# Encoder layer on one core: order of transfers, splits and down-weight sums at the phase boundaries

## What is computed

```
x = x + concat(attention, pooling) @ w_out        # 1024 -> 1024
h2 = rmsnorm(x, norm2_g)
x = x + square(relu(h2 @ w_up)) @ w_down          # 1024 -> 4096 -> 1024
```

## Time and profile before

| | us |
|---|---|
| timed runs | 1613.30, 1613.46, 1616.38 (median 1613.46) |
| profiled execution, its own time | 1616.33 |
| its span | 1614.5 |
| TensorE busy with matmuls | 1517.9 (94%) |
| DVE, ACT, POOL busy | 1027.1, 728.8, 391.0 |

### The profile page before, as it was taken

One profiled execution on the slowest core, in us unless ns is written; L12 is line 12 of the kernel. 1 busy time (PEld: TensorE's weight loads), 2 busy tenths in 40 slices (PEclk: granted clock), 3 DMA queues, 4 the chain that ended last, 5 costly groups with the idle time before them and its releaser, 6 DMA issues.

```text
span 1614.5 us, 23469 instructions
## 1 busy us (share of the span) xinstructions
PE 1517.9 (94%) x8000; PEld 1343.0 (83%) x8000; DVE 1027.1 (64%) x1290; ACT 728.8 (45%) x1231; POOL 391.0 (24%) x337
## 2 busy tenths in 40 slices
PE   7999989999999987999999999997799999999998
PEld 6999867888778867999999999996587777777777
DVE  6434489999866556345454454466587677687675
ACT  5223279999853334445554454544222223223220
POOL 3423667888830000000000000020211211211200
PEclk9999999999999988999999999999799999999999
DMA  6110021000214638433323333347342342442434
GB/s 223 50 38 17 17 79 34 14 13 10 66 69 182 238 127 322 154 121 141 141 104 145 128 128 135 116 179 266 146 156 88 134 155 80 143 144 90 137 98 169
DMA packets 68789, 193.55 MB, mean 120 GB/s; under 512 B 5504, under 2 KB 7680, under 8 KB 68736
## 3 DMA queue, kind: packets, MB, share of 16 engines
q1 hardware_dynamic: 66832, 181.85, 32.2%
q10 hardware_dynamic: 1904, 11.01, 1.6%
HBM read 120.49 MB, written 67.63 MB: 117 GB/s over the span
## 4 chain that ended last, share of the span: by engine, by line
PE 75%; DVE 8%; issue 5%; POOL 4%; ACT 4%; DMA 3%; SPq 0%; DVEq 0%; ACTq 0%; POOLq 0%
PE ps L732 20%; PE ps L733 20%; PE ps L734 20%; PE ps L929 4%; PE ps L830 3%; PE ps L937 2%; DVE yacc L1820 2%; POOL prob L1979 1%; PE ps L845 1%; PE ps L846 1%; PE ps L812 1%; PE ps L814 1%; DMA wdraw<-in_w_down 1%; ACT wdhi L1032 1%; DMA h2d<-stage1b 1%
## 5 line engine op out<-in xcount | busy, mean ns | idle before, releaser
L732 PE MATMUL ps<-h,wuhi 128*128 128x384 f32 x896 | 302.6, 338 | 15.6 <-ACT u L1032 10.6
L732 PE MATMUL ps<-wdhi,hidhi 128*128 128x512 f32 x672 | 266.3, 396 | 38.6 <-DVE yacc L1820 38.6
L733 PE MATMUL ps<-h,wuhi 128*128 128x384 f32 x896 | 302.0, 337 | 0.0
L734 PE MATMUL ps<-h,wulo 128*128 128x384 f32 x896 | 301.7, 337 | 0.0
L733 PE MATMUL ps<-wdlo,hidhi 128*128 128x512 f32 x672 | 264.0, 393 | 0.0
L734 PE MATMUL ps<-wdhi,hidlo 128*128 128x512 f32 x672 | 263.6, 392 | 0.0
L1820 DVE TENSOR_TENSOR yacc<-yacc,ps 128x1024 f32<-128x1024 f32 x168 | 204.3, 1217 | 79.1 <-PE ps L734 78.2
L1032 ACT ACTIVATE hidhi<-hin 128x1024 fp32r<-128x1024 f32 (+1 forms) x72 | 86.5, 1203 | 343.8 <-PE ps L734 343.5
L2069 POOL TENSOR_TENSOR wdraw<-wdraw 128x1024 f32<-128x1024 f32 x8 | 19.2, 2399 | 750.9 <-DMA wdraw<-in_w_down 750.9
L732 PEld LDWEIGHTS ps<-wdhi,hidhi 128*128 128x128 f32 x672 | 127.5, 190 | 72.5 <-DVE yacc L1820 34.3
L732 PEld LDWEIGHTS ps<-h,wuhi 128*128 128x128 f32 x896 | 170.2, 190 | 17.0 <-issue 11.0
(11 more groups left out here) (165 smaller groups left out, 2884.0 us busy)
## 6 DMA issues: line engine op xcount, KB each, us to landing
hd<-hout SPq DMA_DIRECT2D x64, 384.0 KB, 3.3
hin<-hd SPq DMA_DIRECT2D x48, 512.0 KB, 3.7
hd<-hout SPq DMA_DIRECT2D x32, 576.0 KB, 2.8
hin<-hd SPq DMA_DIRECT2D x24, 768.0 KB, 4.4
wuraw<-in_w_up SPq DMA_DIRECT2D x17, 1024.0 KB, 5.9
wdraw<-in_w_down SPq DMA_DIRECT2D x8, 2048.0 KB, 9.9
h<-h2d ACTq DMA_DIRECT2D x7, 1536.0 KB, 11.5
xin<-in_x SPq DMA_DIRECT2D x12, 512.0 KB, 3.3
```

Source lines behind the costliest of these rows:

```text
L732: pe.matmul(out, w_hi, m_hi, start=start, stop=False, skip_group_check=resumed)
L733: pe.matmul(out, w_hi, m_lo, start=False, stop=False, skip_group_check=resumed)
L734: return pe.matmul(out, w_lo, m_hi, start=False, stop=stop, skip_group_check=resumed)
```

## The change

Five things change, none of them a matmul or its place.

1. SP stores the parked pairs one pass earlier and ahead of the residual: in passes 2, 4, 6.
2. ACT, start of the up phase: `load_h2(2)` moves behind `hi_h2(11)`, `load_h2(3)` joins it there, and `save_u(0, 0, 0)` moves ahead of the wait for the last tile.
3. Last up step (s = 31): `hi_wd(0, 0, 0)` and `(0, 0, 1)` come behind `save_u(31, 1, 0)`; the first chunk's four down-weight sums are made by DVE in place of POOL, spread through the step; `hi_wd(0, 0, 2)` and `hi_part(0, 0)` change places among the copies.
4. SP at the start of the down phase: the loads of unit 1, `load_wd(1)` and `load_y(2)` stand ahead of the last `store_hid`. DVE makes the last hidden sums at the end of unit 0 rather than in its middle.
5. Slots of the weight splits. Chunk 0 splits the weights of chunk 1 in units 1 and 2 alone. From chunk 1 on, ACT's copies of blocks 0, 3, 2, 5, 6 stand one part earlier.

```
@@ block.sync
+                if p in (2, 4, 6):
+                    store_h2((p - 2) // 2)
                 store_x2(p)
-                if p in (3, 5, 7):
-                    store_h2((p - 3) // 2)
...
             load_y(1)
-            load_hid(0, 1, 0)
+            for i in range(3):
+                load_hid(0, 1, i)
+            load_wd(1)
+            load_y(2)
             store_hid(last, 0, 0)
-            for i in (1, 2):
-                load_hid(0, 1, i)
-            load_y(2)
@@ block.scalar, up_step
-                save_u(s, par, 0)
-                if loads:
-                    load_h2(3)
+                if not loads:
+                    save_u(s, par, 0)
+                if first_down:
+                    hi_wd(0, 0, 0)
+                    hi_wd(0, 0, 1)
...
                 if first_down:
                     hi_wd(0, 0, 3)
-                    hi_part(0, 0)
                 square_relu(s, par, 1)
...
+                if first_down:
+                    hi_wd(0, 0, 2)
+                    hi_part(0, 0)
                 square_relu(s, par, 2)
...
@@ block.scalar, down_chunk
+                    slots = ((), (0,), ()), ((1, 3), (2,), ()), ((4, 5), (6,), ())
+                    if first:
+                        slots = ((), (), ()), ((), (0, 1), ()), ((3, 2), (4, 5, 6), ())
...
-                            for o in (((), (), (0,)), ((1,), (3,), (2,)), ((4,), (5,), (6,)))[u][i]:
+                            for o in slots[u][i]:
                                 hi_wd(n + 1, 1 - z, o)
...
-            for o in range(3):
+            for o in range(2):
                 load_h2(o)
+            save_u(0, 0, 0)
             act.wait_ge(xs2_done, TT)
             hi_wu(0, SLOTS - 1)
             hi_h2(TT - 1)
+            for o in (2, 3):
+                load_h2(o)
@@ block.vector, up_step
+                if first_down:
+                    lo_wd(0, 0, 1)
+                    for k in (2, 3):
+                        sum_wd(k)
+                    lo_wd(0, 0, 3)
                 sum_u(s, par, 1)
...
+            for k in (0, 1):
+                sum_wd(k)
             up_step(2 * CHUNKS - 1, 1, late=CHUNKS, first_down=True)
@@ block.gpsimd
-            sum_wd(0, 0)
             sum_wd(1, 1)
```

More of the change, by code:

```diff
@@ L684, in _ @@
             load_y(1)
-            load_hid(0, 1, 0)
+            for i in range(3):
+                load_hid(0, 1, i)
+            load_wd(1)
+            load_y(2)
             store_hid(last, 0, 0)
-            for i in (1, 2):
-                load_hid(0, 1, i)
-            load_y(2)
             def load_ahead(n, u, last=False):
-                if u == 0 and not last:
+                if u == 0 and not (isinstance(n, int) and n == 0) and not last:
                     load_wd(n + 1)
@@ L700, in load_ahead @@
                         load_hid(*m, i)
[L702 to L705, removed]
+            for u in range(UNITS):
+                load_ahead(0, u)
+            with sp.Fori(1, DOWNS - 2) as n:
+                for u in range(UNITS):
+                    load_ahead(n, u)
             for n in (DOWNS - 2, DOWNS - 1):
@@ L1386, in hi_part, with down_chunk @@
                 copy(hidhi[i][:], hin[i][:]).then_inc(hid_hi, 1)
-            def down_chunk(n, z, last=False):
+            def down_chunk(n, z, last=False, first=False):
                 for u in range(UNITS):
                     m = UNITS * n + u
+                    slots = ((), (0,), ()), ((1, 3), (2,), ()), ((4, 5), (6,), ())
+                    if first:
+                        slots = ((), (), ()), ((), (0, 1), ()), ((3, 2), (4, 5, 6), ())
                     for i in range(3):
@@ L1437, in _ @@
             hi_wd(0, 0, 6)
-            down_chunk(0, 0)
+            down_chunk(0, 0, first=True)
             down_chunk(1, 1)
@@ L1778, in up_step @@
                     lo_wu(late, 6)
+                if first_down:
+                    lo_wd(0, 0, 0)
                 if prep is not None:
@@ L1788, in up_step @@
                 if first_down:
-                    lo_wd(0, 0, 3)
+                    lo_wd(0, 0, 2)
                 sum_u(s, par, 2)
@@ L1797, in up_step, with sum_wd @@
                     lo_part(0, 0)
-                    lo_wd(0, 0, 2)
+            def sum_wd(k):
+                b11, b12, b21, b22 = (wdraw[:, :, f, h] for f, h in ((0, 0), (0, 1), (1, 0), (1, 1)))
+                dve.wait_ge(wd_in, 16)
+                if k == 1:
+                    dve.wait_ge(up_done, SLOTS * (2 * CHUNKS - 2))
+                if k:
+                    dve.wait_ge(wd_sum, min(k, 2))
+                if k >= 2:
+                    dve.wait_ge(wd_lo, 2)
+                out, a, b, op = ((b12, b22, b12, ALU.subtract), (wd_t2[0][:], b12, b11, ALU.add),
+                                 (b21, b21, wd_t2[0][:], ALU.subtract), (b11, b22, wd_t2[0][:], ALU.subtract))[k]
+                dve.tensor_tensor(out, a, b, op).then_inc(wd_sum, 1)
             def lo_wd(n, z, o):
@@ L1830, in lo_wds @@
                                 lo_wd(n + 1, 1 - z, o)
+                    slots = ((), (), (), (0,)), ((1,), (3,), (2,), ()), ((4,), (), (5,), (6,))
+                    if first:
+                        slots = ((), (), (), ()), ((), (), (0,), (1,)), ((3,), (2,), (4,), (5, 6))
                     accumulate(n, u, 0)
@@ L1843, in down_chunk @@
                         lo_wd(0, 0, 6)
-                    lo_wds(*((), (1,), (4,))[u])
+                    lo_wds(*slots[u][0])
                     accumulate(n, u, 3)
[L1846 to L1849, removed]
+                    lo_wds(*slots[u][1])
                     accumulate(n, u, 4)
@@ L1857, in down_chunk @@
                         lo_part(m + 1, 2)
-                    lo_wds(*((0,), (), (6,))[u])
+                    if first and u == 0:
+                        for k in range(4):
+                            sum_hid(2 * CHUNKS - 1, k)
+                    lo_wds(*slots[u][3])
             up_step(0, 0, prep=1, sums=False)
@@ L2070, in sum_wd @@
                 pool.wait_ge(wd_sum, 4 * n + 1)
[L2071 to L2075, removed]
+                if isinstance(n, int) and n == 1:
+                    for i in range(3):
+                        pool.wait_ge(h_out[i], 32 * CHUNKS)
                 else:
```

10 lines of the change are left out of this document (2 added, 8 removed).

## The result

| | before | changed kernel |
|---|---|---|
| median of the runs, us | 1614.74 (1613.30 to 1616.38, 4 runs) | 1561.66 (1556.85 to 1564.15, 4 runs) |
| profiled execution, us | 1616.33 (span 1614.5) | 1556.85 (span 1555.1) |
| TensorE busy in the span | 1517.9 us, 94% | 1502.7 us, 97% |

The ratio is 0.9667, with a 95% interval of 0.964 to 0.9695: the kernel is 3.3% faster. Timed again later, in five rounds, it took 1558.03 (1556.70 to 1560.42) against 1615.07 for the kernel before, a ratio of 0.9650 (0.9635 to 0.9664). The forecast was 1549.3 in a range of 1542 to 1566, so sign and range hold, and the gain is 53 to 57 us, not the 64 of the sum. Both medians lie above the forecast's own bounds of 1543 to 1557, in the part of the range that it had given to its rivals.

What follows compares the result with a forecast made beforehand. TensorE, busy most of the span, bounds the kernel; only its idle time and lower clock can be won. Terms A to E sum to 64.1 us: 1616.33 to 1552.2 profiled, median 1549.3, range 1542 to 1566.

Steps and rivals of the forecast that it cites:

- the forecast's own bounds: Whole kernel: the forecast with its terms' bounds, 1543 to 1557 us, given a chance of 0.60.
- A: Output projection, pass 9: storing the parked pair earlier removes the whole stall before tile 8's transposes; gain 9.9 us.
- The rival on late residual loads: Output projection: 3.5 MB stores hold `load_x2` over its 5 us margin, A halves or less; 1554 to 1559; chance 0.07.
- B: Start of up phase: earlier `save_u` and fewer transfers beside the up-weight load; gain 3.9 us, bounds 0 and 6.
- C: Last up step: POOL has no sums there and DVE's chain sets the down phase's start; gain 5.5 us.
- D: Chunk 0 of the down phase: `load_wd(1)` no longer waits behind the last `store_hid`; gain 19.4 us, bounds 14 and 22.
- E: Chunks 1 to 6: earlier ACT copies remove both TensorE gaps, 4.23 us a chunk; gain 25.4 us.
- The rival in which POOL keeps DVE out for both: Chunks 1 to 6: POOL's two sums run without a DVE turn, E falls to about 12; time 1563; chance 0.12.
- the hidden part: Chunk 0 rival: unit 2's hidden loads land 6 to 10 us later than +30, D is 10; time 1559; chance 0.15.
- The slower rival: From chunk 1: ACT's block 0 copy waits for weights ahead of `hi_part`; 1617 and up; slower or equal, chance 0.03.

Runs made afterwards that it cites:

- the first experiment on term B: Changed kernel with `load_h2(2)` and `(3)` issued behind ACT's first two copies of the next up weights; weight load 8.7 us rather than 9.8, step 2 1.5 us earlier.

## Why the forecast held, and where it did not

**A, right, 9.9 for 9.9.** The mechanism was the one named: in the changed kernel the stores go out at 542 and `lo_h2(7)` no longer waits for them. The margins on the residual loads held, since passes 8 to 10 start 11.8 apart. Putting the stores back costs 9.4. The rival on late residual loads has fallen.

**B, wrong, 0.1 for 3.9.** The step that failed is "and now it is two. I take 7.5, in the middle". The first part of the term was good: `save_u` earlier brought product 2 1.2 us forward, where I had taken 1. The count of two was wrong: two transfers stood ahead of the load, and the two that the edit moved reached ACT's queue 2.8 and 3.2 us behind its issue, while it was under way, so four ran beside it as before. And 7.5 was a value between two rows with no reason for it (the middle of 5.9 and 10.3 is 8.1). The load took 9.8, after 10.3 before. With this the gap grew to 3.71 instead of shrinking to 1, and the stretch at half clock stayed. The bounds 0 and 6 held it at their end. The 0.1 is of one profile, though: in the three executions of the same order without the stretch, step 2 starts 54.2 to 54.7 after pass 11, a gain of 1.2 to 1.7, still less than half of the term. What would have told is a count of bytes: 3 MB of h2 on ACT's queue ahead of the load and 3 MB behind it, all moved at some 420 GB/s (it takes 9.8 us for 4.1 MB), and not a median of loads that ran with less beside them. The Trainium skill, DMA: Bandwidth & Descriptors, section Issuing engines are not separate DMA queues, agrees: the transfers of ACT's queue and of SP's interleaved, and the lengths of 4.95, 8.7 and 9.8 us show it.

**C, right, 5.6 for 5.5**, product 4 at 11.05 after the step's start where I had 11.2, the down phase at 19.67 where I had 19.8. The sum holds because it counted DVE's chain through and did not add up the gaps: the vanished 2.38 stood beside the sum and not in it, and the experiment with the copies back, where a gap of 0.99 returns and nothing is lost, bears that out.

**D, right in mechanism, 16.4 for 19.4.** Of the 3.0 that are missing, 1.1 is a slip in the forecast's own sum: 57.1 + 3 + 1.7 + 1.0 + 0.8 is 63.6, not 62.5, so the gain should have read 18.3 and the forecast 1550.4. `load_wd(1)` went out at 13.1 us, as forecast at 13, and the wait for it is gone. What is late next was named rightly: the part of unit 2 behind the last `store_hid`. Its landing was sized at +30 and measured 1110.92 + 6.17 - 1084.48 = +32.6; the gap was sized at 3 and is 3.18, because by then TensorE too was later. The reason for that is a second gap, of 1.40 in unit 1, that I had left out, and it is the term of the sum that failed: I let POOL's first sum begin later (weights landed at +23 to +28), and they landed at +20.5. POOL's sum ran from 1104.94, DVE's split beside it took 2.22 instead of 1.22 from 1106.20, and the late sums and the accumulation stood behind that. The term missed a meeting of POOL and DVE that depends on a microsecond.

**E, right but for the first chunk, 24.7 for 25.4.** Chunks 2 to 6 take 57.12, as forecast. The turns of POOL and DVE are as counted:

```profile
1180.46 2.40 POOL L2109 TENSOR_TENSOR wdraw<-wdraw,wd_t 128x1024 f32<-128x1024 f32 x1 [10.20 <-DVE wdlo L1462]
1182.81 3.42 POOL L2110 TENSOR_TENSOR wdraw<-wdraw,wd_t 128x1024 f32<-128x1024 f32 x1
...
1181.88 2.06 DVE L1462 TENSOR_TENSOR wdlo<-wdraw,wdhi 128x1024 fp32r<-128x1024 f32 x1
1183.86 1.21 DVE L1844 TENSOR_TENSOR yacc<-yacc,ps 128x1024 f32<-128x1024 f32 x1
1184.99 2.85 DVE L1462 TENSOR_TENSOR hidlo<-hin,hidhi 128x1536 fp32r<-128x1536 f32 x1
```

DVE's split ends 1.1 us after POOL's first sum, so it had its turn between the two; POOL's second sum is the longer for it (3.42), and DVE's `lo_part` is held in turn (2.85 for 1536 columns, where 1024 take 1.22). The rival in which POOL keeps DVE out for both, a lock passed on within POOL's own list, did not occur. The accumulation between them starts as soon as DVE is free and takes its 1.2 us under POOL's sum. Chunk 1 lost 0.8 at one gap of 0.48.

**The time.** The stages are 3.8 + 3.0 + 0.7 - 0.1 = 7.4 us short of the sum, and the unchanged head was 2.8 us faster, which no edit made; that is 4.6, the distance of the profiled 1556.85 from the 1552.2 on that scale. The rest of the miss is the step from there to a median. I took off 2.9 because the profiled execution before lay that far above its median; the one after lay 4.8 below its own. The other profiled executions that can be set beside a median lay 0.2 to 4.0 us from it, so a single one says to some 5 us where a median will be, and its offset should not be carried over. Whether a set of runs tells 0.2% from no change, as the forecast had it, depends on the set: the 95% intervals here reach 0.15% to 0.28% to either side.

That the range held was in part luck. It had been widened to 1566 for rivals, and none of them occurred: POOL gave DVE its turn, the residual loads came in time, and the hidden part landed 2.6 us late, not 6 to 10. The time fell where they were priced all the same, by the short terms B and D and by the offset. The slower rival, ACT waiting for block 0, had no part: no chunk shows it.

## What to carry to other kernels

Where an engine has a list in fixed order, its waits are won by moving an instruction ahead of one that waits longer, and this is worth most in a loop: one placement, met again in each of six chunks, gave 25 of the 59 us. A transfer's length at a crowded place follows from all the bytes that are under way with it; holding some back brings the first forward and takes the time out of a later one, so look for the wait that it will create. Before a short instruction is moved, ask what stands behind it there: the same 2.1 us of sums stood ahead of a gap of 1.4 in their old place and of one of 2.57 behind a late load.

## What the runs showed of the hardware

- The same 1 MB load took at most 4.95 us alone, 8.7 with 3 MB issued 5.4 us ahead of it, and 9.8 with 3 MB more issued 2.8 us behind it, with the DMA engines full at 416 to 433 GB/s.
- A GpSimd instruction and a VectorE one whose two inputs are both in SBUF take turns, and in these rows the first to start goes on while the other stands: DVE's 0.7 us sum took 2.50, its 1.2 us splits 2.06 and 2.23, POOL's 2.4 us sum 3.33 to 3.42. Whoever comes second loses the other's remaining time, and with the weights landing 1.4 us later one chunk took 63.0 us instead of 60.8. An accumulation, which reads PSUM, kept its 1.21 us beside POOL (1183.86). The Trainium skill, SBUF — State Buffer, section SBUF: two separate sides, calls it an exclusive lock held for the whole instruction, and these rows agree.
- TensorE's clock after a short gap isn't the same each time. The first pass of the output projection has the same code in all these kernels and took 11.6 to 13.9 us. In the two executions below it follows a gap of 1.27 us; it ran at a granted clock of 1.00 in the changed kernel and 0.78, in part on the 1.2 GHz level, in the first experiment on term B, 2.3 us longer:

```profile
457.15:468.72 11.57, 11.21 (x49) 8.94 (x49) 11.51 (x11) 3.22 (x5) 1.09 (x1) 1.00 0.04 4
```

```profile
458.67:472.55 13.88, 13.88 (x49) 11.17 (x49) 11.49 (x11) 3.22 (x5) 1.08 (x1) 0.78 0.18 65
```

What decides it stays open. It is not the DMA load: the higher share of the second row (0.18 for 0.04) lies behind the pass's first 8 us, in which the share is 0.00 in both while the clock is already 1.00 in the one and 0.50, then 0.73, in the other. Nor do the 4 us ahead of the pass differ in what the engines do: TensorE is busy 1.49 and 1.48 us of them and the DMA share is 0.51 in both.

The stretch of 1.6 us behind product 4 of the first step came and went in the same way. In the seven executions whose orders up to there are the changed kernel's, it is there in the four whose first pass took 11.6 to 12.5 us and not in the three whose first pass took 13.3 to 13.5; no run explains the link. So an edit there of under 2 us can't be judged by one execution.
